# A 2-layer streaming trunk on one core: first weight pairs interleaved k group by k group, x loaded in five pieces, first norm moved

## The reference

```
def rms_norm(x, g):
    y = x * lax.rsqrt(jnp.mean(x * x, -1, keepdims=True) + EPS)
    return y * g

def retention_pool_mixer(h, pos, S0, pool_buf, w_in, ...):
    proj = h @ w_in                       # (320, 2048) @ (2048, 5120)
    q, k, v, g, u = split(proj)           # 8 heads of 128 each for q, k, v, g
    q = rotary(q, pos)
    k = rotary(k, pos) * (RET_DK ** -0.5)
    ...                                   # chunked retention per head, head_rms, * silu(g)
```

## Time and profile before

| | |
|---|---|
| median of three executions | 2922.85 us (2922.36 to 2924.69) |
| span of the profiled execution | 2920.6 us |
| its own time as a run | not among the three shown; the span is 2.25 us under their median |
| TensorE busy | 2863.4 us, 98% |
| VectorE, ScalarE, GpSimd busy | 1594.0, 1027.5 and 141.0 us |
| TensorE in the first 40 us | busy 15.44 us |
| DMA | 412.40 MB read, 143 GB/s over the span |

### The profile page before, as it was taken

How to read it: one execution, slowest core, us unless ns; L and a number is a source line. 1 busy time by engine, 2 the same in 40 slices (tenths; PEclk the granted TensorE clock), 3 DMA queues, 4 the chain that set the end, 5 groups by cost and what they waited for, 6 DMA issues and landing times.

```text
span 2920.6 us, 50149 instructions
## 1 busy us (share of the span) xinstructions
PE 2863.4 (98%) x19211; PEld 2825.0 (97%) x19211; DVE 1594.0 (55%) x2208; ACT 1027.5 (35%) x1122; POOL 141.0 (5%) x154
## 2 busy tenths in 40 slices
PE   6999999999999999999899999999999999999997
PEld 6999999999999999999899999999999999999997
DVE  6666645555455544554656656545554455545553
ACT  3343333333333333333433333333333333323332
POOL 2000021000000000002100000120000000000002
PEclk9999999999999999999999999999999999999999
DMA  5444344444444444444333433444444444444443
GB/s 198 133 141 139 128 150 145 149 149 149 151 150 145 150 151 149 147 146 152 128 115 126 132 114 125 136 150 145 150 151 148 148 150 151 147 148 146 156 144 111
DMA packets 119031, 419.59 MB, mean 144 GB/s; under 512 B 13360, under 2 KB 17712, under 8 KB 118832
## 3 DMA queue, kind: packets, MB, share of 16 engines
q1 hardware_dynamic: 118960, 418.58, 43.4%
HBM read 412.40 MB, written 6.13 MB: 143 GB/s over the span
## 4 chain that ended last, share of the span: by engine, by line
PE 95%; DVE 3%; ACT 1%; issue 0%; POOL 0%; DMA 0%; DVEq 0%; SPq 0%; ACTq 0%; POOLq 0%
PE gb L425 91%; PE ab L431 4%; DVE w_lo L925 1%; DVE a_lo L932 0%; PE ab L443 0%; ACT w_hi L695 0%; DMA raw<-in_weights 0%; DVE work L1432 0%; POOL sq_one L385 0%; DVE work L1496 0%; ACT a_hi L702 0%; POOL sq_sum L387 0%; DVE work L1042 0%; DVE work L1085 0%; DVE work L1338 0%
## 5 line engine op out<-in xcount | busy, mean ns | idle before, releaser
L925 DVE TENSOR_TENSOR w_lo<-raw,w_hi 128x1024 fp32r<-128x1024 f32 x772 | 951.1, 1232 | 1218.3 <-ACT w_hi L695 1217.3
L695 ACT ACTIVATE w_hi<-raw 128x1024 fp32r<-128x1024 f32 x772 | 818.3, 1060 | 1724.6 <-PE gb L425 1722.4
L425 PE MATMUL gb<-a_hi,w_hi 128*128 128x320 f32 x4240 | 1325.9, 313 | 28.0 <-DVE a_lo L932 19.3
L425 PE MATMUL gb<-a_lo,w_hi 128*128 128x320 f32 x4240 | 1313.3, 310 | 0.0
L425 PE MATMUL gb<-a_hi,w_lo 128*128 128x320 f32 x4240 | 1313.3, 310 | 0.0
L425 PEld LDWEIGHTS gb<-a_hi,w_hi 128*128 128x128 f32 x4240 | 799.0, 188 | 38.4 <-DVE a_lo L932 19.5
L425 PEld LDWEIGHTS gb<-a_lo,w_hi 128*128 128x128 f32 x4240 | 799.0, 188 | 2.0 <-issue 0.2
L425 PEld LDWEIGHTS gb<-a_hi,w_lo 128*128 128x128 f32 x4240 | 798.8, 188 | 0.0
L425 PE MATMUL gb<-b_hi,w_hi 128*128 128x320 f32 x1920 | 593.7, 309 | 1.6 <-DVE b_lo L1197 1.6
L425 PE MATMUL gb<-b_lo,w_hi 128*128 128x320 f32 x1920 | 593.3, 309 | 0.0
L425 PE MATMUL gb<-b_hi,w_lo 128*128 128x320 f32 x1920 | 593.3, 309 | 0.0
(11 more groups left out here) (154 smaller groups left out, 839.4 us busy)
## 6 DMA issues: line engine op xcount, KB each, us to landing
raw<-in_weights SPq DMA_DIRECT2D x772, 512.0 KB, 3.3
x<-in_x SPq DMA_DIRECT2D x4, 640.0 KB, 8.0
out_y<-work SPq DMA_DIRECT2D x4, 640.0 KB, 3.3
out_c<-work SPq DMA_DIRECT2D x8, 257.0 KB, 4.5
work<-in_ret_tables SPq DMA_DIRECT2D x8, 160.0 KB, 3.3
work<-in_w_pool SPq DMA_DIRECT2D x1, 1024.0 KB, 13.9
out_ret<-work SPq DMA_DIRECT2D x8, 128.0 KB, 3.4
work<-in_ml_state SPq DMA_DIRECT2D x8, 128.0 KB, 4.1
```

The costliest lines, as they stand in the source:

```text
L425: last = nc.tensor.matmul(bank(b, m), w[:, at:at + P], v[:, t:t + T], start=kg == k == n == 0, stop=kg == groups - 1 and k == UK - 1 and n ...
L695: nc.scalar.activation(w_hi[:, at:at + UW], raw[:, at:at + UW], ACT.Copy).then_inc(hi_ready, 1)
L925: V.tensor_tensor(w_lo[:, at:at + UW], raw[:, at:at + UW], w_hi[:, at:at + UW].bitcast(F32), ALU.subtract).then_inc(lo_ready, 1)
```

## The change

Six edits, all in the first 100 us:

1. SyncE loads the norm gains (16 columns of `cols`) first, x in five pieces (2, 2, 4, 4 and 4 tiles in place of four times 4) between the first four units, and the other columns of `cols` behind the constants.
2. The first eight units are ordered k by k in memory: u0 is kg 0 of the q/k pair, u1 kg 0 of the v/g pair, u2 kg 1 of q/k, and so on. TensorE fills both bank pairs in turn, so one k group of x serves two units. q/k is complete after u6, v/g after u7.
3. ScalarE and VectorE alternate two tiles of x with one unit.
4. The squares for the first norm are made by ScalarE, 4 tiles an instruction (`first_sq`), and added by VectorE in four steps of halving width. GpSimd has no part in the first norm. TensorE's product with ones comes after u8 and is one in place of two.
5. VectorE takes q and k of head 0 out with the plain cos and sin tables (`first_qk`), and multiplies them by `rt` afterwards (`first_qk_scaled`). The scores of head 0 come after u10.
6. Head 0's steps sit at other units: v turned after u10, sums after u12, square sum after u13, head 1's scores after u15. ScalarE loads the table with the square root at its start.

The core of the diff:

```
+            sp.dma_start(cols[:, 0:KT], cols_in[:, 0:KT]).then_inc(mix_loaded, 16)
+            load_x(0, 0, 2)
+            load(Unit(0))
+            load_x(1, 2, 2)
+            load(Unit(1))
+            load_x(2, 4, 4)
+            load(Unit(2))
+            load(Unit(3))
+            load_x(3, 8, 4)
+            load_x(4, 12, 4)
             sp.dma_start(con[:], consts_in).then_inc(con_loaded, 16)
+            sp.dma_start(cols[:, KT:], cols_in[:, KT:]).then_inc(cols_loaded, 16)
...
-            pool.wait_ge(x_loaded[0], 16)
-            pool.wait_ge(x_loaded[1], 16)
-            squares(0, 0, KT // 4, loaded=True)
...
-            head(0, None, False)
-            with pe.Fori(0, HEADS - 1) as i:
-                head(i + 1, i, True)
+            for kg in range(4):
+                pe.wait_ge(a_ready, 2 * kg + 2)
+                unit(Unit(2 * kg), kg, 4, a_hi, a_lo, 0)
+                unit(Unit(2 * kg + 1), kg, 4, a_hi, a_lo, 1)
+            for j in range(8):
+                q, kg = divmod(j, 4)
+                unit(Unit(8 + j), kg, 4, a_hi, a_lo, q, q + 1)
+                if j == 0:
+                    first_norm()
+                if j == 2:
+                    ret_scores_of(0)
+                    ret_turn_v(0)
+                if j == 4:
+                    ret_sums(0)
+                if j == 5:
+                    ret_square_sum(0)
+                if j == 7:
+                    ret_scores_of(1)
+            with pe.Fori(0, HEADS - 2) as i:
+                head(i + 2, i)
...
+            nc.scalar.preload_act_table(ACT.Sqrt)
+            for q in range(4):
+                a_upper(2 * q, "mix0", x_loaded[q + 1 if q else 0], 16)
+                split(Unit(2 * q))
+                a_upper(2 * q + 1, "mix0", x_loaded[q + 1], 16)
+                split(Unit(2 * q + 1))
+                nc.scalar.activation(first_sq[:, q * 4 * T:(q + 1) * 4 * T], x[:, q * 4 * T:(q + 1) * 4 * T],
+                                     ACT.Square).then_inc(first_squares, 1)
...
+            def first_qk():
+                ret_rotated(0, 7, con[:, CON["cos"]:CON["cos"] + T], con[:, CON["sin"]:CON["sin"] + T])
+                V.tensor_tensor(q_t, q_t, q_swap, ALU.add)
+                V.tensor_tensor(k_t, k_t, k_swap, ALU.add).then_inc(qk_raw, 1)
+
+            def first_qk_scaled():
+                dve.wait_ge(qk_raw, 1)
+                V.tensor_tensor(q_t, q_t, rt[:], ALU.mult)
+                V.tensor_tensor(k_t, k_t, rt[:], ALU.mult).then_inc(qk_ready, 1)
+                dve.wait_ge(qk_ready, 1)
...
+            dve.wait_ge(mix_loaded, 16)
+            for q in range(4):
+                a_lower(2 * q, "mix0", 2 * q + 1)
+                split(Unit(2 * q))
+                a_lower(2 * q + 1, "mix0", 2 * q + 2)
+                split(Unit(2 * q + 1))
+            split(Unit(8))
+            dve.wait_ge(first_squares, 4)
+            w = 8 * T
+            step.inc(V.tensor_tensor(first_sq[:, 0:w], first_sq[:, 0:w], first_sq[:, w:2 * w], ALU.add))
+            own()
+            split(Unit(9))
+            dve.wait_ge(con_loaded, 16)
+            first_qk()
+            for w in (4 * T, 2 * T):
+                step.inc(V.tensor_tensor(first_sq[:, 0:w], first_sq[:, 0:w], first_sq[:, w:2 * w], ALU.add))
+                own()
+            V.tensor_tensor(first_sq[:, 0:T], first_sq[:, 0:T], first_sq[:, T:2 * T], ALU.add).then_inc(first_sum, 1)
+            split(Unit(10))
```

More of the change, by code:

```diff
@@ L176, in trunk_kernel @@
         heads_only = used[0]
+        first_sq = work[:, heads_only + 5 * T:heads_only + 5 * T + 16 * T]
         q_t, k_t, q_swap, k_swap, cos_r = (piece(T) for _ in range(5))
@@ L387, in add_square, with squares @@
                 step.inc(nc.gpsimd.tensor_tensor(sq_sum[:], sq_sum[:], sq_one[:], ALU.add))
-            def squares(norm, pair, pairs=KT // 2, loaded=False):
-                if norm:
+            def squares(norm, pair, pairs=KT // 2):
+                if norm > 1:
                     pool.wait_ge(norm_sum, norm)
@@ L431, in small, with first_norm @@
                 return nc.tensor.matmul(out, lhs, rhs, start=start, stop=stop)
+            def first_norm():
+                pe.wait_ge(con_loaded, 16)
+                pe.wait_ge(first_sum, 1)
+                small(ab[:, 0, 0:T], ones, first_sq[:, 0:T]).then_inc(norm_sum, 1)
             def norm(k, more=((con_loaded, 16),)):
-                pe.wait_ge(sq_done, k + 1)
+                pe.wait_ge(sq_done, k)
                 pe.wait_ge(*more[0])
@@ L495, in ret_tail, with head @@
                     ret_square_sum(h)
-            def head(h, i, tail):
+            def head(h, i):
                 for j in range(8):
                     q, kg = divmod(j, 4)
[L500 to L511, removed]
+                    unit(Unit(16 + j, i, 8), kg, 4, a_hi, a_lo, q, i * 2 + (q + 3))
+                    ret_tail(h - 1, j)
                     if j == 6:
                         ret_scores_of(h)
-            head(0, None, False)
-            with pe.Fori(0, HEADS - 1) as i:
-                head(i + 1, i, True)
+            for kg in range(4):
[18 more added lines that the diff above has]
+                head(i + 2, i)
             pe.wait_ge(w_pool_loaded, 16)
@@ L953, in _, with ret_rotated, ret_qk @@
             half = slice(0, P // 2), slice(P // 2, P)
-            def ret_qk(h, units):
+            def ret_rotated(h, units, cos, sin):
                 used(units)
                 for dst, swap, m in ((q_t, q_swap, 0), (k_t, k_swap, 1)):
-                    V.tensor_tensor(dst, bank(0, m), cos_r, ALU.mult)
-                    V.tensor_tensor(swap[half[0], :], bank(0, m)[half[1], :], sin_r[half[1], :], ALU.mult)
-                    last = V.tensor_tensor(swap[half[1], :], bank(0, m)[half[0], :], sin_r[half[0], :], ALU.mult)
+                    V.tensor_tensor(dst, bank(0, m), cos, ALU.mult)
+                    V.tensor_tensor(swap[half[0], :], bank(0, m)[half[1], :], sin[half[1], :], ALU.mult)
+                    last = V.tensor_tensor(swap[half[1], :], bank(0, m)[half[0], :], sin[half[0], :], ALU.mult)
                 last.then_inc(pair_taken, 1)
                 dve.wait_ge(pair_taken, h * 2 + 1)
+            def ret_qk(h, units):
+                ret_rotated(h, units, cos_r, sin_r)
                 V.tensor_tensor(q_t, q_t, q_swap, ALU.add)
@@ L1078, in _ @@
+            split(Unit(10))
             for j in range(8):
-                split(Unit(AHEAD + j))
+                split(Unit(8 + AHEAD + j))
                 if j == 0:
[L1082 to L1090, removed]
@@ L1095, in _ @@
                 if j == 4:
+                    ret_tail(0, 3, stored=False)
+                if j == 5:
                     own()
-                    ret_qk(0, 4)
+                    ret_qk(1, 12)
+                if j == 6:
+                    ret_tail(0, 6)
                 if j == 7:
[L1099 to L1106, removed]
+                    ret_tail(0, 7)
```

111 lines of the change are left out of this document (53 added, 58 removed).

## The result

| | before | changed |
|---|---|---|
| median | 2922.71 us (4 runs, 2922.36 to 2924.69) | 2905.49 us (4 runs, 2904.92 to 2907.32) |
| ratio | | 0.9942, 95% interval 0.9930 to 0.9955 |
| span of the profiled execution | 2920.6 us | 2904.1 us |
| TensorE busy | 2863.4 us | 2860.0 us |
| first matmul | 15.97 | 9.10 |

The changed kernel is 17.2 us faster by the medians, 16.5 by the spans. The forecast was 2906.8, a difference of 16.1. The common point is where both kernels have done the same TensorE work; it came 16.2 us earlier, against 16.1 forecast.

A forecast was written before the change was run, and what follows sets the result against it. TensorE, 95% of the chain, bounds the kernel, with 22.3 us of waits at the start. 41.2 + 8 x 3.58 + 0.25 + 0.54 + 5.64 = 76.2 against 92.3; 2922.85 - 16.1 = 2906.8 us, range 2904.0 to 2911.0.

The forecast's parts named there:

- When the data land: SyncE's load queue at 400 KB a us: gains at 3.9, x's first piece at 5.0, u4 at 22.8.
- The first k groups: Splits on ScalarE and VectorE: first matmul at 9.7 against 15.97, a stop of 0.3 ahead of u4.
- The new wait: u8 waits for first_qk on VectorE: starts at 41.2 after TensorE stood 0.75; norm's product waits 0.25 and costs 0.54.
- The unknown durations: In u8's chain: a square of 1280 columns taken as 1.2 us, the addition over 2560 columns as 2.9.
- Covered work: Head 0's steps finish before TensorE needs them: q and k 50.6, due 52.8; v 60.6, due 61.5.
- The cover called the narrowest: cos and sin, u12, v and g done at 53.7, due at 54.0; if gone, it costs what it exceeds.
- The sum: u8's start, eight units, norm's product and small products: common point at 76.2 against 92.3, 16.1 us less.
- the lower bound: VectorE's chain early, TensorE the limit: u8 at 39.0 with half the slow matmuls, 2.2 us less, 2904.6; with spread 2904.0.
- The pieces did bring the first matmul forward: Rival denied it: x, u0 or gains land late, TensorE starts at 15.97, only 10.9 less, 2912.0; 12%.
- The clock did not fall at the three short stops: Rival: clock falls at stops of 0.3, 0.75 and 0.25; one or two relapses of 1.8 us, 2908.6 to 2910.4; 12%.
- Nothing was given back later: Rival: a later stage not paced by TensorE loses 10.3 us again, 2917 to 2923; 3%.

The follow-up runs named there:

- (5): Changed kernel with edit 5 undone, q and k of head 0 behind the first norm: common point 85.1, median 2915.24 us against 2905.49.
- (8): Changed kernel with GpSimd doing eight unused products and eight sums on its own tile: common point 77.4, median 2906.55 us.
- (9): Changed kernel without the call that loads the square root's table first: common point 76.7, median 2906.41 us.
- (1): Changed kernel with the 1024 KB load of w_pool moved from in front of u4 to behind u7: common point 74.5, median 2904.18 us.
- (2): Changed kernel with u0 to u7 in the old order, x's tiles split ahead of u4: common point 74.4, median 2904.82 us.
- (6): Kernel before with edit 1's loads alone: common point 90.0 against 92.2, median 2920.34 us.
- (7): Kernel before with only the first norm's squares moved to ScalarE and VectorE: common point 85.7, median 2914.39 us.
- (10): Kernel before with edit 1's loads and the squares moved, old order of units, q and k behind the norm: common point 84.6, median 2914.81 us.
- (3): Changed kernel with old order of u0 to u7 and w_pool behind u7 together: common point 75.2, median 2903.84 us.
- (4): Changed kernel with old unit order, w_pool behind u7, and the first unit asking for two tiles of x first: common point 74.9, median 2904.69 us.

## Why the prediction was right, by its own steps

**When the data land: right, and closer than it had a claim to.** u4 landed at 22.7 (22.8 forecast), w_pool 13.5 after its issue. That it came within 0.1 us is in part luck: with the same loads ScalarE started u4 at 22.99 in (5), 23.18 in (8) and 23.33 in (9). x's first piece came at 4.4, not 5.0: the gains landed 1.8 us after their issue, where 3.1 from a 64 KB load was taken, and x's first 320 KB took 3.2. The Trainium skill (DMA: Bandwidth & Descriptors, Specifications) has a read-modify-write for transfers under 512 bytes. The load in rows of 64 bytes was over at about 2.5 and cost nothing that the trace shows.

**The first k groups: right, 0.6 early.** First matmul at 9.10 (9.7), which is the early landing. ScalarE waited 6.45 us for u4. The stop ahead of u4 was 0.7 (0.3): TensorE was early by 0.6, so it only waited longer. By the rows, an x that came at 5.0 would have changed nothing at u4, since TensorE would have stood 0.6 less; no run delays x by just that. (8) delays the first matmul by 2.3 us, more than the stops can hide, and 1.4 arrive.

**The new wait: right in place and size.** u8 started at 40.92 (41.2) behind VectorE's last instruction on q and k. The unknown durations: a square of 1280 columns 1.26, started 1.16 before the next instruction (1.2), the addition over 2560 columns 2.82 (2.9). TensorE stood 0.6 (0.75). The norm's product and its wait took 0.74 together (0.79). The claim that this chain hangs on u4's landing and that only short stops hang on it is what (1) tested and (9) happened to show: a u4 that came 2.2 earlier gave 1.5 and no more, one that came 0.6 later moved everything by its delay.

**Covered work: right, with more room than computed.** v was ready at 57.5, due at 61.2 (60.6 and 61.5): the weighing had been priced at its upper bound. The cover called the narrowest, v and g out of PSUM before u12, was 1.5 us (52.6 against 54.17) where 0.3 had been forecast. The Tanh load ended before its gate's data came, and nothing waited for it. The Trainium skill's drain behind a table load (ScalarE: Activation LUTs, What ACT_TABLE_LOAD costs) was again not seen: in (9) the load starts at 46.13 and the root follows at 47.42, 1.29 later.

**The sum: 76.2 forecast, 76.04 measured.** (Its terms add up to 76.27, and by its own terms the 39.0 in the lower bound is 39.2; neither matters here.) The difference to before is 16.2. It is 16.1 at the long run of TensorE that starts at 480.53 before and at 464.43 after, and 16.45 from 1480 us on. The waits after 100 us are the same in both profiles, but for one of 0.8 that is 1.9 after the change and whose end moved with the rest. Around it the lower clock falls in different places: 36 matmuls take 7.08 us before and 8.29 after the change, and 24 later on 5.26 and 3.71. The balance is the 0.3 by which the spans differ more than the common point. The 17.2 of the medians lies within what executions of one kernel differ by (2.4 us among the four of the changed kernel).

**The rivals.** The pieces did bring the first matmul forward. The clock did not fall at the three short stops: at 0.7, 0.6 and 0.2 us they were shorter than the stop of 1.99 after which it had kept its rate before, and the granted clock is 1.00 around them. It did fall in (5), after 7.0 us. Nothing was given back later.

**What the forecast did not see.** It took the diff as a whole and left open what the interleaving brings. In this kernel it brings nothing: (2) is 1.6 us earlier at the common point without it. What it would bring with remainders at 1.05 us was not tried. The gain consists of x's remainders at half the time, a first matmul 6.9 us earlier, and no wait for the norm. Of these only the last keeps the others: (6), (7) and (10) all start earlier than the kernel before (10.10, 13.52, 10.18) and lose all or part of it in a stop of 10.0, 4.3 and 8.0 us for the squares. Undoing edit 5 alone takes back 9.0 of 16.2.

(1) to (4) are ahead of the changed kernel by 1.1 to 1.6 us at the common point, except (3) at 0.9, and by 0.7 to 1.7 in the medians. Only for (1) do the executions lie apart as well: 2903.15 to 2904.71 against 2904.92 to 2907.32. Those of (2), (3) and (4) overlap with the changed kernel's. So w_pool behind u7 is the one step further that is likely real; which of the four is best stays open.

## What to carry to other kernels

At the start of a kernel, list every wait of the bounding engine up to the first point at which both versions have done the same work, and build that point from each engine's stream. A first matmul several us earlier means little if a later wait is set by another chain. A factor that can be applied after the first use of a result can take a whole chain (squares, sum, root, reciprocal) off the path; here that was worth more than any other edit tried. Order the loads by what waits for them: 1 MB that is needed 300 us later stood in front of a unit that everything waited for.

## What the runs showed of the hardware

- The number of matmuls at the low rate at the start, the first one counted, differed from trace to trace with no stop in between: 12 in (5) and (10), 13 in (1) and (9), 14 in (2), 15 before and after the change, 18 in (7), 19 in (3) and (6), 21 in (4), 22 in (8). At 0.12 us each that is 1.2 us, more than the differences between (1) and (4). These are different kernels with one trace each, so no run here shows how much one kernel varies. The Trainium skill (TensorE: Matmul & The Clock Gate, Part 1) says that this number varies from run to run of the same kernel. The granted clock reads 1.00 in these stretches; the slow start shows only in the distances of the starts.
- After stops of 4.3 (7), 6.3 (before), 7.0 (5), 8.0 (10) and 10.0 us (6) TensorE came back at the low rate; after 1.4 (6) and 1.99 (before) it did not. The granted clock (the third value from the end, 1.00 at full rate) shows it, for the kernel before in the ten us around its stop of 6.3, and for (5) right behind its stop:

```profile
30.00:40.00 10.00, 3.73 (x15) 2.69 (x14) 9.59 (x12) 0.00 (x0) 0.00 (x0) 0.69 0.22 65
```

```profile
48.00:54.00 6.00, 5.84 (x22) 5.87 (x23) 3.31 (x6) 0.00 (x0) 0.00 (x0) 0.52 0.44 134
```

- ScalarE's first table load waited for whatever stood in front of it in the stream: it ran at 0.74 where no wait for data was in front of it, at 2.50 behind the gains' load in (9), and at 7.81 behind a weight unit in the kernel before.
- GpSimd working beside VectorE made VectorE slower: a remainder of x took 1.05 us with GpSimd squaring x, 1.00 with GpSimd on a tile of its own (8), and 0.55 with GpSimd silent, after the change and in (7).
